# Layer modulation rows summed on VectorE instead of TensorE in a two-block network

## What is computed

```python
c_act = silu(c)                                   # one vector of 1024
for l in range(2):
    mod = c_act @ w_mod[l] + b_mod[l]             # 6144 = 6 vectors of 1024
    sh1, sc1, g1, sh2, sc2, g2 = split(mod, 6)
    h = rms_norm(x) * (1 + sc1) + sh1
    x = x + g1 * hybrid_mixer(h, ...)             # attention, RG-LRU, gates, w_out
    h = rms_norm(x) * (1 + sc2) + sh2
    x = x + g2 * (swiglu(h) if l == 0 else moe_swiglu(h))
```

## Time and profile before

| what | us |
|---|---|
| three runs | 2806.57, 2813.26, 2814.1 |
| their median | 2813.26 |
| the profiled execution, span from first to last instruction | 2807.6 |
| PE busy in it | 2740.4 (98%) |
| DVE busy in it | 2005.1 (71%) |
| ACT busy in it | 1675.2 (60%) |
| mixer 0, PE's first product to the end of wo | 41.8 to 314.0 |
| FFN of layer 0 | 322.0 to 502.4 |
| mixer 1 | 510.9 to about 771 |

### The profile page before, as it was taken

One profiled execution on the slowest core, in us unless ns is written; L12 is line 12 of the kernel. 1 busy time (PEld: TensorE's weight loads), 2 busy tenths in 40 slices (PEclk: granted clock), 3 DMA queues, 4 the chain that ended last, 5 costly groups with the idle time before them and its releaser, 6 DMA issues. The chain is left out here.

```text
span 2807.6 us, 39565 instructions
## 1 busy us (share of the span) xinstructions
PE 2740.4 (98%) x15736; PEld 2320.1 (83%) x15736; DVE 2005.1 (71%) x2112; ACT 1675.2 (60%) x1983; POOL 19.5 (1%) x44
## 2 busy tenths in 40 slices
PE   7999999999999999999999999999999999999998
PEld 5878999788978888888888888888867898867897
DVE  3766655586688989989898989986565556474555
ACT  3575544557467777777777777775454445353544
POOL 0000000000000000000000000001000000000000
PEclk8999999999999999999999999999999999999999
DMA  9847553856589999999999999985423454414452
GB/s 337 298 149 257 180 207 110 308 189 210 166 301 369 345 350 364 347 366 342 371 342 349 364 348 365 341 298 178 150 92 133 175 206 146 173 67 150 168 199 75
DMA packets 311131, 693.97 MB, mean 247 GB/s; under 512 B 7255, under 2 KB 26181, under 8 KB 310997
## 3 DMA queue, kind: packets, MB, share of 16 engines
q1 hardware_dynamic: 309184, 689.60, 68.5%
q0 software_dynamic: 1200, 2.29, 0.5%
q10 hardware_dynamic: 612, 0.18, 0.0%
HBM read 690.99 MB, written 1.05 MB: 246 GB/s over the span
## 5 line engine op out<-in xcount | busy, mean ns | idle before, releaser
L2704 DVE TENSOR_TENSOR ring_rest<-ring,weights_hi 128x2048 fp32r<-128x2048 f32 x270 | 608.5, 2284 | 10.1 <-ACT weights_hi L2031 8.3
L2031 ACT ACTIVATE weights_hi<-ring 128x2048 fp32r<-128x2048 f32 x270 | 516.7, 1916 | 135.7 <-PE ps L1762 71.0
L1760 PE MATMUL ps<-weights_hi,xg_hi 128*128 128x512 f32 x1008 | 402.3, 399 | 2.1 <-DVE xg_lo L2704 1.2
L1762 PE MATMUL ps<-weights_hi,xg_lo 128*128 128x512 f32 x1008 | 395.3, 392 | 0.0
L1761 PE MATMUL ps<-ring_rest,xg_hi 128*128 128x512 f32 x792 | 307.9, 389 | 0.0
L2031 ACT ACTIVATE arena<-ps 128x512 f32<-128x512 f32 (+6 forms) x307 | 157.3, 529 | 220.4 <-PE ps L1762 54.1
L1781 PE MATMUL ps<-weights_hi,hidden_split_moe 128*128 128x512 f32 x1008 | 282.9, 392 | 1.5 <-DVE hidden_split_moe L2704 1.2
L2704 DVE TENSOR_TENSOR ring_rest<-ring,mix_hi 128x2048 fp32r<-128x2048 f32 (+2 forms) x76 | 171.0, 2254 | 126.5 <-ACT mix_hi L2031 125.8
L2704 DVE TENSOR_TENSOR w_split<-ring,w_split 128x1024 fp32r<-128x1024 f32 x128 | 150.9, 1221 | 151.1 <-ACT w_split L2031 151.1
L2704 DVE TENSOR_TENSOR late_rest<-arena,weights_hi 128x2048 fp32r<-128x2048 f32 x108 | 245.4, 2285 | 5.5 <-ACT weights_hi L2031 4.3
L2031 ACT ACTIVATE weights_hi<-arena 128x2048 fp32r<-128x2048 f32 x108 | 206.9, 1917 | 65.4 <-PE ps L1762 35.5
(11 more groups left out here) (307 smaller groups left out, 5344.2 us busy)
## 6 DMA issues: line engine op xcount, KB each, us to landing
ring<-in_moe_w_gate_dram SPq DMA_DIRECT2D x54, 2048.0 KB, 8.0
ring<-in_moe_w_up_dram SPq DMA_DIRECT2D x45, 2048.0 KB, 8.0
ring<-in_moe_w_down_dram SPq DMA_DIRECT2D x36, 2048.0 KB, 7.9
ring<-in_mlp_w_dram SPq DMA_DIRECT2D x32, 2048.0 KB, 9.0
arena<-in_moe_w_down_dram SPq DMA_DIRECT2D x27, 2048.0 KB, 8.0
ring<-in_w_mod_dram SPq DMA_DIRECT2D x48, 1024.0 KB, 9.0
ring<-in_w_in_dram SPq DMA_DIRECT2D x48, 1024.0 KB, 5.9
arena<-in_moe_w_up_dram SPq DMA_DIRECT2D x18, 2048.0 KB, 8.0
```

The lines of the kernel that those rows point to most:

```text
L1760: pe.matmul(b, xg_hi[:, k, :], hi[:, i, :], start=(k == 0), stop=False)
L1762: mm = pe.matmul(b, xg_lo[:, k, :], hi[:, i, :], start=False, stop=(k == KD - 1))
L2031: return act.activation(o, i, func, **kw)
L2704: return dve.tensor_tensor(o, a, b, op)
```

## The change

The 20 chunks are no longer multiplied by PE. DVE makes the row in place (`add_rows`): for the eight blocks of 128 rows of `w_mod` it does one linked operation of 128x512 each, `part = w[:, k] * c_act[:, k]` for the first and `part = w[:, k] * c_act[:, k] + part` for the other seven; for a gate one more operation on 1x512 adds the bias row. What is left is one row per partition; PE sums over the 128 partitions (`sum_rows`) with four one-column matmuls against a column of ones, or for a gate with one 512-column matmul of a tile of ones. ACT's copy of the partial rows is gone.

The chunks are spread anew: six in each mixer, eight in the FFN of layer 0. A mixer's half chunks are summed after `rest_of_piece` 3, 4, 5, 6, 16 to 19, 24, after the emptying of ya's first two banks, after 26 and after 27. In the FFN two operations follow each `in` step and three each `out` step, so that the 64 are spread over the first 28 steps. Their weights no longer pass SP's ring: POOL loads halves of 1 MB into two buffers in turn. Its first load waits for the end of yl, the second for the end of wo, each later one for the reading of the half two before it. Two more row buffers are added.

Ring slots that held a half chunk are free when DVE has read it (`mod_half_read`), no longer when PE has.

```diff
+MIX_MODS = {0: chunks_of((0, 3), (0, 4), (0, 2)), 1: chunks_of((1, 4), (1, 2), (1, 5))}
+FFN_MODS = chunks_of((0, 5), (1, 0), (1, 1), (1, 3))
+MOD_LOAD_AT = ("qkv0", "qkv1", "sg0", "sg1", "sg3", "ya0")
+MOD_SUM_AT = ("xr0", "xr1", "sg1", "sg3", "ya1", "yl1")
...
+                readers = [stream.last_read[b] for b in stream.before[n]]
+                by_pe = [value[key] for key in readers if key[0] != "read"]
+                by_dve = [halves_read(*key[1:]) for key in readers if key[0] == "read"]
...
+                        if n < 2:
+                            pool.wait_ge(pe_done, value["wo", 0, TT - 1] if n else value["yl", 0, 3])
+                        else:
+                            pool.wait_ge(sem("mod_half_read"), 2 * len(MIX_MODS[0]) + n - 1)
...
+            def sum_rows(chunk):
+                part = rows_of(chunk)
+                pe.wait_ge(sem("mod_half_read"), halves_read(chunk, 1))
+                b = open_bank(("mf", *chunk))
+                if chunk[1] in (2, 5):
+                    done(pe.matmul(b, ones, part, start=True, stop=True))
+                else:
+                    done(mod_columns(b, part, ones[:, 0:1]))
...
+                    if k == 0:
+                        link(ts(part, w[:, j], cact[:, k:k + 1], ALU.mult))
+                        continue
+                    ins = stt(part, w[:, j], cact[:, k:k + 1], part, ALU.mult, ALU.add)
...
                 for c in range(2):
                     rest_of_piece(25 + 2 * c)
+                    if c:
+                        add_rows_of(l, 5, 1)
                     for j in range(2 * c, 2 * c + 2):
                         b = full(dve, ("ya", l, j))
...
+                    if c == 0:
+                        add_rows_of(l, 4, 1)
                     rest_of_piece(26 + 2 * c)
+                    if c == 0:
+                        add_rows_of(l, 5, 0)
```

More of the change, by code:

```diff
@@ L299, in __init__ @@
             if l == 0:
-                for kind, j in ffn_steps():
+                for n, (kind, j) in enumerate(ffn_steps()):
+                    for chunk in ffn_sums_at(n):
+                        self.add(("mf", *chunk), "act")
                     if (kind, j) == ("out", FT // 2 - 1):
@@ L368, in product @@
                      "dve" if name in ("ya", "yl") else "act")
[L370 to L376, removed]
+        for chunk in mods_at(MOD_SUM_AT, l, f"{name}{c}"):
+            self.add(("mf", *chunk), "act")
     def hidden(self, name, at, n):
@@ L551, in __init__ @@
         self.at = {key: n for n, key in enumerate(self.items)}
[L553 to L557, removed]
     def mix(self, name, l, c):
@@ L561, in mix @@
             self.add((name, l, c, half), mix_done_key(l, MIX_AT[name, c] + half))
+        for chunk in mods_at(MOD_LOAD_AT, l, f"{name}{c}"):
+            for half in range(2):
+                self.add(("mod", *chunk, half), ("read", chunk, half))
     def add(self, key, last_read):
@@ L1175, in _ @@
                     load(gb[0:1, i], I["b_mod"][l:l + 1, v * D:(v + 1) * D], "gates_landed")
+                if l == 0:
+                    for n, (layer, v, c, r) in enumerate((*chunk, r) for chunk in FFN_MODS for r in range(2)):
+                        if n < 2:
+                            pool.wait_ge(pe_done, value["wo", 0, TT - 1] if n else value["yl", 0, 3])
+                        else:
+                            pool.wait_ge(sem("mod_half_read"), 2 * len(MIX_MODS[0]) + n - 1)
+                        first, a = D // 2 * r, v * D + c * 512
+                        load(mod_ffn[n % 2], I["w_mod"][layer][first:first + D // 2]
+                             .rearrange("(k p) n -> p k n", p=P)[:, :, a:a + 512], f"mod_ffn_{n % 2}_landed")
             pool.wait_ge(sem("merged"), L)
@@ L1457, in mod_rows, with mod_columns, modulation @@
                 done(mm)
[L1459 to L1463, removed]
[L1464 to L1480 removed]
+            def mod_columns(b, rows, column):
+                for i in range(4):
+                    mm = pe.matmul(b[:, i:i + 1], rows[:, i * P:(i + 1) * P], column, start=True, stop=True)
+                return mm
+            def sum_rows(chunk):
[6 more added lines that the diff above has]
+                    done(mod_columns(b, part, ones[:, 0:1]))
+            def modulation(l, point):
+                for chunk in mods_at(MOD_SUM_AT, l, point):
+                    sum_rows(chunk)
             memory_uses = [0]
@@ L2244, in _ @@
                     round_piece(n + 4)
-                    modulation(l, c)
+                    modulation(l, f"qkv{c}")
                 act.wait_ge(emptied["act"], taken[0])
@@ L2410, in _ @@
                     for n, (kind, j) in enumerate(steps_ffn):
+                        for chunk in ffn_sums_at(n):
+                            keep_sum(chunk)
                         if n + 2 < len(steps_ffn):
```

198 lines of the change are left out of this document (110 added, 88 removed).

## The result

The changed kernel takes 2843.12 us (median of four runs, 2839.61 to 2846.26) against 2811.99 before (four runs); the ratio is 1.011, with a 95% interval of 1.0089 to 1.0131. It is 31 us slower. The forecast was 14 us slower, 2827: the sign and the wide range (2797 to 2846) held, the forecast's own range (2813 to 2840) did not, and the size was off by more than a factor of two. In the profiled executions the spans are 2839.5 and 2807.6, 31.9 apart, and they can be compared stage by stage.

The account below looks back on a forecast made before the run. The prediction took PE (busy 98%) as the bound, with DVE nearly as close in two mixer stretches: PE does 45 us less, waits bring back 59, sum +14.0, so 2827 us, own range 2813 to 2840, wide range 2797 to 2846.

Parts of the forecast that it names:

- Term 5: FFN's entry: first up load issued only at wo's end, so PE waits longer between wo and FFN, +17.1 us.
- term 6: FFN's start: the long idle stretch drops PE to half clock behind it, +2.6 us, ends 0 and 4.
- Term 7: Between FFN and mixer 1: mixer 1's first load gets the slot of the FFN's last step, +3.0 us.
- Terms 1 to 4: PE's waits in each mixer: LRU gates +5.4, after sg's first product +3.1, ya's start +2.1, yl's second bank +7.5 us.
- term 8: FFN's steps: DVE's added operations just fit its idle time; +0.5 us for late loads.
- Rival C: FFN starves as ring loads stretch POOL's landing from 8.7 to 13 us: +28, 2855 us; chance 0.12.
- Rival B: Mixers stay bound by PE, terms 1 to 4 (36.2 us) vanish: -22.2, 2791 us; chance 0.13.
- rival D: Half of the mixers' waits come: -4.1, 2809 us; chance with E together 0.27.
- Rival E: First up load isn't the FFN's wait, 17.1 and 2.6 us go away: 2808 us; chance with D together 0.27.

Follow-up runs that it names:

- before_slots: The kernel before with only the FFN's slot order changed, so its first gate and up load get the slots of wo's pieces: 2829.99 us, ratio 1.0055.
- after_slots: The changed kernel with the FFN's loads in slots 0, 1, 2, 3, 4 instead of 2, 3, 0, 1, 4: 2817.01 us, ratio 1.0014.
- slots_yl: after_slots with each mixer's last half chunk summed on DVE after the emptying of ya's banks 2 and 3, not before: 2808.47 us, ratio 0.9982.
- before_dummy: The kernel before with four needless one-column matmuls on PE ahead of eight of the FFN's 22 in steps: 2819.26 us, ratio 1.0024.
- gates_busy: slots_yl_sg with 11 needless matmuls on PE ahead of the first LRU gates of each mixer: 2796.19 us, ratio 0.9936.
- before_sg: The kernel before with only ACT's order changed, second LRU gates' sigmoids ahead of the rounding of piece 18: 2814.28 us, ratio 1.0004.
- slots_yl_sg: slots_yl with ACT's sigmoids of the second LRU gates ahead of the rounding of piece 18 in both mixers: 2797.49 us, ratio 0.9939.

## Why the prediction was right in sign and wrong in size

**Right.** The work on DVE: a half chunk takes 3.1 us, forecast 2.9. Term 5, the FFN's entry: forecast +17.1 (with term 6, +19.7), measured +18.5, and before_slots and after_slots show it from both sides. Term 7, mixer 1's first load: +3.0, measured +2.7. Terms 1 to 4: 18.1 us of waits a mixer, measured +18.4 and +18.0. What PE loses, forecast 32.2 and 20.8, is 33.0 and 22.6 when the modulation's matmuls are added up in the two traces, from the start of each to the start of the next. The mixers' 1588 other matmuls are the same in both kernels; added up in the same way they take 5.6 us more in mixer 0 and 7.7 more in mixer 1. So the balance closes: -33.0 + 18.4 + 5.6 = -9.0 (measured -9.1), and -22.6 + 18.0 + 7.7 = +3.1 (measured +3.1).

**Wrong: term 6, the clock.** The prediction took one cold start, at the FFN's entry, because the one wait that it had seen lose the clock was 6.33 us long. It forecast eight waits of 2.1 to 7.5 us in the mixers and put the slowed work behind them at nothing. Halving the busy time at half clock gives 8.3 us more in mixer 0, 7.3 in mixer 1, 5.1 ahead of the experts and 2.9 at the entry: 23.6 instead of 2.6. This estimate can't simply be added to the forecast, which missed the span by 17.9 us in all: 5.0 and 5.8 in the mixers, 3.0 ahead of the experts, 5.8 in the FFN, less 1.6 elsewhere. What the lengths show is the 5.6 and 7.7 of the mixers' unchanged matmuls, 13.3 together, where the forecast had nothing; the 3.0 ahead of the experts; and 1.4 at the entry (26.5 for 25.1), where it had 2.6. The 13.3 are not all clock: other matmuls ran at the faster of the two paces below more often than before, in mixer 0 for 1.4 us.

The norm's windows had the hint in the kernel before: the norm ahead of the experts has idle stretches of about 1 us only, and 3.4 us at half clock behind them. The same stage shows that a fallen clock costs time and isn't only a mark beside a wait. Its instructions are the same in all thirteen kernels, and it takes 25.4 us where 3.4 us of it are at half clock (two traces), 26.7 to 27.4 with 6.8 (eight), 27.1 with 10.2 (one) and 28.3 or 28.4 with 13.7 (two). Two of them:

```profile
771.24:796.67 25.43, 21.77 (x171) 20.80 (x170) 19.19 (x74) 10.90 (x19) 0.00 (x0) 0.93 0.90 331
```

```profile
770.65:798.95 28.30, 26.20 (x171) 25.54 (x170) 19.31 (x74) 10.89 (x19) 0.00 (x0) 0.76 0.80 297
```

The first is the kernel before, the second slots_yl. 10.2 us more at half clock cost 3.0 there, since waits of PE in the stage shrank from 3.7 to 2.1 at the same time. How much of this stage's 3.0 is due to the change is open: of the nine kernels with the change two have 13.7 us at half clock, one 10.2 and six 6.8, and 6.8 is also what before_slots and before_dummy have, without the change. That gates_busy isn't slower with its needless PE work shows nothing of the clock: that work lies in idle time.

**Wrong: a term that is missing in the FFN.** The FFN takes 13.9 us more, not 8.1. The eight sums take 6.2 (forecast 7.6) and the waits ahead of them 1.8 (term 8 had 0.5), together just the forecast's 8.1. The other 6.0 are a slower pace of the ordinary matmuls, 281 ns in the mean instead of 276, which no term had; after_slots has 3.4 of it, and before_sg 5.8 without any sum.

```profile
L1691 PE MATMUL ps<-hT_hi_ffn,w_in_ffn 128*128 128x256 f32 x704 | 126.5, 281 | 0.0
...
L1485 PE MATMUL ps<-arena 128*128 128x1 f32 x48 | 6.0, 246 | 0.9 <-DVE arena L2722 0.9
L1494 PE MATMUL ps<-arena 128*128 128x512 f32 x4 | 2.1, 618 | 0.9 <-DVE arena L2716 0.9
```

Rival C, the starved FFN, didn't happen: DVE waits there for POOL once, 0.3 us, and its loads land in 7.4 us (median of 14), less than the 8.7 of the earlier trace rows. The Trainium skill's estimate of 4.4 us ("DMA: Bandwidth & Descriptors", section "Anatomy of one DMA — SWDGE (gpsimd) path") is too low for both rows; that C has no chance, which the prediction worked out from it, came true all the same. Rival B, mixers bound by PE, would have needed the waits away, and rival D half of them; they came whole, and even slots_yl_sg keeps 3 us at the gates. Rival E is refuted by the rows of the FFN's entry and by before_slots.

**The missing margin** of the forecast's own range (2813 to 2840) was thus one-sided: the ends given for term 6 were 0 and 4, for the slowed work in the mixers alone 13.3 came, and no end allowed for the FFN's pace.

## What to carry to other kernels

When a change shortens the busy engine and lets others set the pace, count each new wait twice: once as idle time, once for the work behind it at half clock (here 36.4 us of new waits in the mixers came with 13.3 us of slower matmuls, an estimate of the price from one pair of traces); then look for the order of loads, banks and roundings that makes the wait, since three small mends of order turned +31 us into -15 without moving any work back, and 17 needless matmuls a mixer brought it to -21. Where slots are shared in rotation, changing the number of items that pass through shifts every later owner: recompute what each later load has to wait for. Needless matmuls in an idle gap that can't be removed cost nothing as long as they fit into it; whether they pay isn't sure: a gap cut to 0.6 us kept the clock, gaps cut to 1.9 and 3.8 lost it, and gaps of 2.3 and 2.4 us kept it.

## What the runs showed of the hardware

**The clock falls at short waits, but not at each.** In the changed kernel, in the mixers and at mixer 1's start, eight of the ten waits over 1.8 us (1.9 to 7.7) went with 3.4 or 6.8 us of granted clock 0.50, beginning in the wait or just behind it; 1.87 and 2.87 us did not. Counted over the mixers of all thirteen traces, a stretch at 0.50 began in the wait or within 3.5 us of its end for 32 of the 33 waits of 3.2 us and more, for 20 of the 37 between 1.8 and 3.2, and for 5 of the 66 between 1.0 and 1.8. The same wait of the same program can go either way (2.5 us in the kernel before kept the clock, 2.48 in before_slots lost it); what else decides isn't told by these runs. The Trainium skill, page "TensorE: Matmul & The Clock Gate", section "🔬 Part 1: The HAM clock gate (the "warmup" mystery)", says that a gate passes half or all of PE's clock pulses by how busy PE has been; the trace agrees in that only 0.50 and 1.00 occur. By the same page of the Trainium skill such a ramp costs under 1% of a typical kernel; here the estimate by halving, 23.6 us more than before, is 0.8% of 2839.5 us. It agrees, and yet it is three quarters of the size of the 31 us that were to be forecast.

**Matmuls have two paces at the full clock.** In the FFN 256-column matmuls of the same line follow each other every 113 to 114 ns or every 117 to 118, 512-column ones every 229 or every 233.5: 4 ns each, at a granted clock of 1.00. A pace lasts for tens of microseconds to a whole stage. That of the 256-column matmuls changes in before_dummy at each of the eight breaks in the run of matmuls, in the changed kernel at four of eight, in after_slots at three, and in none of them elsewhere in the FFN. All nine kernels with such breaks in the FFN had 288 or more slow ones there, and of the four without a break three had 9. The fourth is before_sg. Its FFN has not one instruction changed, and it ran wholly at the slow pace, 186.1 us instead of 180.3. The mean of the group below is 276 ns in the kernel before; here it is of before_sg, then of before_dummy:

```profile
L1672 PE MATMUL ps<-hT_hi_ffn,w_in_ffn 128*128 128x256 f32 x704 | 126.1, 281 | 0.7 <-issue 0.7
```

```profile
L1675 PE MATMUL ps<-hT_hi_ffn,w_in_ffn 128*128 128x256 f32 x693 | 122.5, 279 | 0.0
```

So 6 us of any difference in this stage can be chance, and part of the spread of the kernel before's runs (2806 to 2820) may be this. Breaks change the pace; what sets it at the start of a stage stays open: no run here held it fixed.
